# Differential attention one unit later, norms that share one root tile, and another order in the stage that rotates and norms the convolution

## The reference

```python
def diff_attention(q, k, v, lam):                       # layers 0 and 1 of the first block
    s = einsum('bqhpd,bkhpd->bhpqk', q, k) * 64 ** -0.5  # two score maps for each of 4 heads
    p = softmax(s, -1)
    a = p[:, :, 0] - lam * p[:, :, 1]
    return einsum('bhqk,bkhe->bqhe', a, v)
def rms_norm(x, w):
    return x * rsqrt(mean(square(x), -1) + eps) * w      # also with the mean taken off first (layer norm)

# first block, each layer
o = rms_norm(diff_attention(...), subln_w) * (1 - lam_init)      # per head of 128 features
# second block, layer 0 (even_mixer)
q = (rms_norm(cq, q_norm) @ w_uq).reshape(B, T, 8, 96)
kv = rms_norm(ckv, kv_norm) @ w_ukv
q, k = rms_norm(q, q_g), rms_norm(k, k_g)                        # per head of 96 features
q, k = rope on the last 32 features of each head
o_conv = silu(layer_norm(depthwise_conv(a * sigmoid(gate), dw_w) + dw_b, ln_g, ln_b))
# second block, layer 1 (odd_mixer)
q, k = rms_norm(q, q_g), rms_norm(k, k_g)                        # 8 heads of 64 features
y = head_group_norm(y0 + y1, gn_g, gn_b) * gate                  # with the mean taken off
```

## Time and profile before

| | |
|---|---|
| median of 3 runs | 3100.18 us (3095.39 to 3105.36) |
| profiled execution | 3105.21 us, span 3103.4 us |
| mean granted TensorE clock | 0.934 of full |
| busy | PE 2679.9 us (86%), DVE 1347.8 (43%), ACT 486.5 (16%) |
| DMA | 651.32 MB, mean 210 GB/s |

### The profile page before, as it was taken

How to read it: one execution, slowest core, us unless ns; L and a number is a source line. 1 busy time by engine, 2 the same in 40 slices (tenths; PEclk the granted TensorE clock), 3 DMA queues, 4 the chain that set the end, 5 groups by cost and what they waited for, 6 DMA issues and landing times. The chain is left out here.

```text
span 3103.4 us, 45313 instructions
## 1 busy us (share of the span) xinstructions
PE 2679.9 (86%) x19830; PEld 1647.8 (53%) x19830; DVE 1347.8 (43%) x2526; ACT 486.5 (16%) x1173; POOL 26.4 (1%) x48
## 2 busy tenths in 40 slices
PE   6988999999987999998969989879969787766665
PEld 3457844446766888735543334345449686423322
DVE  1774388543473876586321101121476763100001
ACT  1023200000222000235221001020051401100000
POOL 0000000000000000000000000000000000000000
PEclk8999999999998999998979999989989898878878
DMA  8530255332341666120239999981110026799998
GB/s 346 191 136 1 85 213 214 142 159 109 112 186 69 244 271 247 67 82 29 83 125 426 427 428 427 428 333 31 43 35 29 2 82 238 305 428 427 427 427 343
DMA packets 66357, 651.32 MB, mean 210 GB/s; under 512 B 14705, under 2 KB 25585, under 8 KB 26481
## 3 DMA queue, kind: packets, MB, share of 16 engines
q1 hardware_dynamic: 66160, 648.43, 51.9%
HBM read 644.08 MB, written 4.33 MB: 209 GB/s over the span
## 5 line engine op out<-in xcount | busy, mean ns | idle before, releaser
L369 PE MATMUL ps<-HT,ring 128*128 128x256 f32 (+1 forms) x3024 | 905.0, 460 | 27.2 <-DMA ring<-in_w_in 9.5
L369 PEld LDWEIGHTS ps<-HT,ring 128*128 128x128 f32 x3024 | 576.1, 192 | 330.9 <-issue 269.4
L2024 PE MATMUL ps<-ring,arena 128*32 128x256 f32 (+1 forms) x2976 | 371.9, 503 | 107.4 <-DMA ring<-in_moe_w 104.7
L442 DVE SCALAR_TENSOR_TENSOR acc<-ring,sil,acc 128x512 f32<-128x512 f32 x616 | 411.7, 744 | 0.0
L369 PE MATMUL ps<-arena,ring 128*128 128x256 f32 (+3 forms) x1232 | 372.3, 463 | 3.2 <-PEq L644 2.0
L2024 PEld LDWEIGHTS ps<-ring,arena 128*32 128x32 f32 (+1 forms) x2976 | 141.0, 130 | 315.8 <-issue 199.7
L369 PEld LDWEIGHTS ps<-arena,ring 128*128 128x128 f32 (+2 forms) x1232 | 230.2, 188 | 137.8 <-issue 118.0
L945 DVE SCALAR_TENSOR_TENSOR XT<-ps,modcols,XT 128x256 f32<-128x256 f32 x148 | 66.6, 481 | 358.3 <-PE ps L369 230.2
L2045 PE MATMUL ps<-ring,arena 128*32 128x256 f32 x960 | 89.9, 539 | 62.3 <-DMA ring<-in_moe_w 62.3
L2045 PE MATMUL ps<-ring,conv 128*64 128x512 f32 x512 | 116.1, 597 | 26.3 <-DMA ring<-in_moe_w 25.7
L369 PE MATMUL ps<-ring,HT 128*128 128x512 f32 (+1 forms) x288 | 105.1, 523 | 0.0
(11 more groups left out here) (379 smaller groups left out, 2618.6 us busy)
## 6 DMA issues: line engine op xcount, KB each, us to landing
ring<-in_moe_w SPq DMA_DIRECT2D x186, 2048.0 KB, 25.6
ring<-in_w_mod SPq DMA_DIRECT2D x24, 2048.0 KB, 8.2
ring<-in_ada_w SPq DMA_DIRECT2D x24, 2048.0 KB, 8.0
ring<-in_w_up SPq DMA_DIRECT2D x16, 2048.0 KB, 12.3
ring<-in_w_down SPq DMA_DIRECT2D x16, 2048.0 KB, 12.5
ring<-in_w_in SPq DMA_DIRECT2D x10, 2048.0 KB, 10.3
ring<-in_od_w_in SPq DMA_DIRECT2D x6, 2048.0 KB, 25.6
arena<-in_moe_w SPq DMA_DIRECT2D x10, 1024.0 KB, 8.0
```

The costliest lines, as they stand in the source:

```text
L369: last = nc.tensor.matmul(bank_of(job, j), lhsT, rhs, start=n == 0, stop=n == len(terms) - 1)
L442: ins = nc.vector.scalar_tensor_tensor(out=acc, in0=weights[:, k, :], scalar=s, in1=acc, op0=ALU.mult, op1=ALU.add)
L2024: last = nc.tensor.matmul(K.ps[M * j:M * j + M, 2 * (e % 2) + i, 0:FW], xs[:, e // 4 % 2, e % 4, 4 * h + k, :], weights((m, e, h), k, slic ...
```

## The change

1. Differential attention: the transposes, the copy out of PSUM, the values and the output copy of a unit each move one round later, and the order inside a round changes. PE: transposes of unit i-3, scores of unit i, values of unit i-4. ACT: copy of unit i-3, then exponentials of unit i. DVE: output of unit i-5. A wait of DVE on the exponentials of unit i-4 is dropped.
2. Norms: groups are gathered in batches (2, then up to 4 each; one each where the divisor differs). New constants `one_sums` and `pair_sums` (38 columns each, nonzero in columns 6 and 7) are cut at an offset, so that group j of a batch adds its sums into rows 2j and 2j+1 of each strip of one common tile. One square root and one reciprocal then serve the batch. A spread takes its row from 64 partitions instead of 128, and where the group has one sum per token it writes 128 output partitions at once instead of 64, so that 4 instructions spread 512 tokens where 8 did; the 512 columns lie in two half-used PSUM banks. On DVE the batch's last group is scaled after the next batch's reciprocal.
3. Rotation and convolution norm: PE packs the third pack before it adds the squares, and spreads the root before the last pack. ACT does its squares and the root before the first `keep`, and does two of the `keep`s after the SiLUs. DVE inverts before the third rotation and scales before the fourth.

The diff at its core:

```diff
-                half = grp["ones"][:, 48:80]
+                rows = grp["sums"][0:block.shape[0], 6 - row:38 - row]
...
-                for c in range(grp["src"][0].shape[1] // P):
-                    for h in range(2):
-                        pick = K.ident[:, 32 * c + 16 * h:32 * c + 16 * h + 1].broadcast_to([P, 64])
-                        last = nc.tensor.matmul(K.ps[64 * h:64 * h + 64, bank, c * P:(c + 1) * P], pick, rows, start=True, stop=True)
+                halves = 2 if grp["sums"] is K.pair_sums else 1
+                for c in (0, 2, 1, 3) if grp["src"][0].shape[1] == TT else (0, 1):
+                    tile = slice(c // 2 * 64, c // 2 * 64 + 64)
+                    for h in range(halves):
+                        at, m = 32 * c + row + h, P // halves
+                        last = nc.tensor.matmul(K.ps[m * h:m * h + m, 2 + 2 * (g % 3) + c // 2, c % 2 * P:(c % 2 + 1) * P],
+                                                K.ident[tile, at:at + 1].broadcast_to([64, m]),
+                                                rows[tile], start=True, stop=True)
...
+    if groups[0]["inv"] != groups[-1]["inv"]:
+        batches = [[g] for g in range(G)]
+    else:
+        batches = [list(range(min(2, G)))] + [list(range(g, min(g + 4, G))) for g in range(2, G, 4)]
...
+            for b in range(B + 1):
+                groups_before = batches[b - 1] if b else []
+                for g in groups_before[:-1]:
+                    scale(g)
+                if b < B:
+                    dve.wait_ge(*K.at("roots_done", b + 1))
+                    nc.vector.reciprocal(root[:, b % 4], root[:, b % 4]).then_inc(*K.inc("inverted"))
+                for g in groups_before[-1:]:
+                    scale(g)
...
-            for i in range(U + 3):
+            for i in range(U + 4):
+                if 3 <= i <= U + 2:
+                    j = i - 3
+                    pe.wait_ge(*K.at("probs_done", 2 * (j + 1)))
...
-                if i >= 3:
-                    j = i - 3
+                if i >= 4:
+                    j = i - 4
...
-                    if i >= 4:
-                        dve.wait_ge(*K.at("exps_done", 2 * (i - 3)))
...
             unpack(0)
+            pack(2)
             for b in range(4):
                 pe.wait_ge(*K.at("squares_act", b + 1))
                 add_up(b, sq[:, b, :]).then_inc(*K.inc("squares_summed"))
-            pack(2)
             unpack(1)
+            pe.wait_ge(*K.at("inverted", 1))
+            spread(root).then_inc(*K.inc("roots_spread"))
             pack(3)
             unpack(2)
-            pe.wait_ge(*K.at("inverted", 1))
-            spread(root).then_inc(*K.inc("roots_spread"))
             unpack(3)
```

More of the change, by code:

```diff
@@ new lines, in _ @@
+                    spread(g, 2 * g, means).then_inc(*K.inc("means_spread"))
+            for b, batch in enumerate(batches):
+                if b >= 2:
+                    pe.wait_ge(*K.at("roots_done", b - 1))
+                for j, g in enumerate(batch):
+                    if b and j == 2:
+                        spread_batch(b - 1)
+                    for i, s in enumerate(groups[g]["src"]):
+                        k = firsts[g] + i
+                        pe.wait_ge(*K.at("squares_" + sides[k], sides[:k + 1].count(sides[k])))
+                        add_up(g, row_of[g], sum_bank(b), sq[0:s.shape[0], k % 4, 0:s.shape[1]], k == firsts[batch[0]],
+                               k == firsts[batch[-1] + 1] - 1).then_inc(*K.inc("squares_summed"))
+                if b and len(batch) <= 2:
+                    spread_batch(b - 1)
@@ L691, in _, with take_roots @@
+            spread_batch(B - 1)
         @block.scalar
         def _(act):
+            def take_roots(b):
+                act.wait_ge(*K.at("squares_summed", firsts[batches[b][-1] + 1]))
+                if b >= 4:
+                    act.wait_ge(*K.at("roots_spread", batches[b - 4][-1] + 1))
+                grp = groups[batches[b][0]]
+                nc.scalar.activation(root[:, b % 4], K.ps[:, sum_bank(b), 0:P], ACT.Sqrt, bias=grp["eps"], scale=grp["inv"]).then_inc(*K.inc("roots_done"))
@@ L766, in _ @@
         def _(pe):
-            for i in range(U + 3):
+            for i in range(U + 4):
+                if 3 <= i <= U + 2:
+                    j = i - 3
+                    pe.wait_ge(*K.at("probs_done", 2 * (j + 1)))
+                    if j:
+                        pe.wait_ge(*K.at("probsT_done", j))
+                    for c in range(len(units[j]["v"])):
+                        last = nc.tensor.matmul(K.ps[:, 6, c * P:(c + 1) * P], E[:, j % nb, 0, c * P:(c + 1) * P], scaled_ident[:, j % 4],
+                                                start=True, stop=True)
+                    last.then_inc(*K.inc("transposed"))
                 if i < U:
@@ L1608, in scaled_norm_stage @@
     n = n_seg * T
-    norm_stage(K, [dict(src=[K.XT[:, k, 0:n] for k in range(KD)], ones=K.ones, inv=1.0 / D, eps=K.eps["rms"],
+    norm_stage(K, [dict(src=[K.XT[:, k, 0:n] for k in range(KD)], sums=K.one_sums, inv=1.0 / D, eps=K.eps["rms"],
                         out=[(K.HT[:, k, SEGS[s]], K.XT[:, k, SEGS[s]], SEGS[s], K.gain[:, s, k:k + 1], mod(K, which, s, k))
```

177 lines of the change are left out of this document (79 added, 98 removed).

## The result

The changed kernel takes 3092.5 us (median of 20 runs, 3087.6 to 3099.3), the kernel before 3100.2 us (20 runs beside them). The ratio is 0.9970, 95% interval 0.9962 to 0.9978: 9 us faster by the ratio (7.6 by the medians), where 26.8 were forecast. The direction was right; the time lies above the range. The profiled execution has a span of 3090.9 us, 12.5 less than before; that of before lay 5.0 us above its median, so part of the 12.5 is chance.

The account below looks back on a forecast made before the run. The last chain is DMA-led experts' work that starts earlier by whatever is saved before it. Terms sum to 26.8 us: 3105.2 becomes 3078.4, and 3073.4 us since that execution lay 5.0 above the median; range 3062 to 3087.

Parts of the forecast that it names:

- attention, layer 0: Differential attention, 16 units, 49.30 us: three steady heads at 0.8 and a shorter drain save 4.0 us (bounds 0, 5.5).
- attention, layer 1: Differential attention, 8 units, 33.48 us: later values shorten the drain and the third round, saving 3.2 us (bounds 1.5, 4.5).
- 16 groups: Norm of 16 groups, 29.04 us: shared reciprocals and shorter spreads, 3.8 us a batch, save 6.0 us (bounds 0, 8.5).
- four of 512: Norm of four groups of 512 tokens, 12.20 us: two of four reciprocals go, spreads halve; saves 2.2 us.
- four of 256: Norm of four groups of 256 tokens, 10.13 us: spreads no shorter; saves 1.2 us.
- low rank: Norm of low-rank inputs, 11.22 us, each group its own batch: earlier root, shorter first spread; saves 1.3 us.
- two with one group: Two norms with 512 tokens and one group: the one spread falls from 1.98 to about 1.0 us; saves 2.0 together.
- 8 groups: Norm of eight groups, 14.34 us: SP's wait for the move to DRAM limits the saving to 2.1 us at most.
- mean off: Norm with the mean off, 12.74 us: two reciprocals and a mean row four times narrower; saves 1.5 us.
- rotation: Rotation and convolution norm, 21.65 us: earlier root, SiLUs ahead of two `keep`s; ends 3.3 us earlier (bounds 1.5, 5).
- the fourth rival: Low clock outlives the norms into the attention behind the rotation stage, costing up to 50 us: 3123 us; chance 0.03.
- Rival 2: Norms leave PE less to do; 16 groups at 1.2 GHz lose 6, other norms 1 more: 3080 us; chance 0.12.

Follow-up runs that it names:

- before_warm: Kernel before plus the same unread products at the same places as in warm; 0.9967 of the kernel before, 3089.4 us.
- warm: Changed kernel plus unread 128x128 products: 5 at each norm's start, 2 ahead of and 2 behind its last spread, 10 in each differential attention; 0.9912, 3078.5 us.
- warm_again: warm run once more with no edit; 0.9942 of the kernel before, 3079.5 us.
- after_again: Changed kernel run once more with no edit; 0.9967 of the kernel before, 3088.2 us.
- warm_rotation: warm_output plus 5 unread products in the rotation and convolution norm, between the sums of squares and the unpack of group 1; 0.9907, 3072.9 us.
- warm_output: warm with VectorE's attention output copy right behind the same round's maxima, and no unread products in the two mean-off layer norms; 0.9924, 3076.1 us.
- unbatched: Changed kernel with each norm group in a batch of its own, spreads over 64 partitions kept; 1.0012 of the kernel before, 3104.5 us.
- unbatched_warm: unbatched plus the unread products of warm; 1.0018 of the kernel before, 3104.8 us.
- warm_ends: Changed kernel with only 2 unread products ahead of each norm's last spread and 2 behind it; 0.9963 of the kernel before, 3089.9 us.

## Why the prediction was wrong

The table has the terms of the sum; the change of each stage in the changed kernel's two traces; the same with filler in the changed kernel alone; and with filler in both kernels (`before_warm` against `warm`, or `warm_again` in two rows), with the clocks of the two. All in us.

| stage | forecast | after, after_again | filler in the changed one | filler in both (clocks) |
|---|---|---|---|---|
| attention, layer 0 | -4.0 | -0.7, -2.4 | -3.5 (`warm`) | -2.47 (1.00, 1.00) |
| attention, layer 1 | -3.2 | -1.9, -3.2 | -2.8 (`warm`) | -1.55 (0.95, 0.94) |
| 16 groups | -6.0 | -6.3, -6.4 | -7.6 (`warm`) | -9.20 (0.84, 1.00) |
| four of 512 | -2.2 | -1.3, -1.5 | -2.8 (`warm_again`) | -1.25 (1.00, 1.00) |
| four of 256 | -1.2 | -0.5, -0.2 | -1.9 (`warm`) | -0.39 (1.00, 1.00) |
| low rank | -1.3 | -1.1, -1.1 | -1.3 (`warm_again`) | -0.46 (1.00, 1.00) |
| two with one group | -2.0 | -0.8, -2.1 | -4.1 (`warm`) | -0.75 (0.83 and 0.86, 0.85 and 0.86) |
| 8 groups | -2.1 | -0.4, +0.5 | -2.1 (`warm`) | -2.02 (1.00, 1.00) |
| mean off | -1.5 | +0.9, +1.7 | -0.1 (`warm`) | -3.47 (0.72, 0.87) |
| rotation | -3.3 | -3.9, -2.9 | -4.3 (`warm_rotation`) | -3.94 (0.73, 0.86) |

Two steps failed. The first stands in the fourth rival and in the sum: "the dense stretches of before are back at full clock at once", and "no part is taken back later". The changed kernel spent 8.8 us at 1.2 GHz in the first norm (6.8 before) and 4.8 us more at the start of the out projection, 7.3 and 2.9 in the 8 groups and the start of the stage behind (3.4 and 0 before), 11.7 in the norm with the mean off (3.8 before). I worked out most stages at the clock of their old row. But the change takes work from TensorE in stages where it already waited, and there the clock went down with it; over all eleven stages the low-clock time stayed (89 and 91 us) while their length fell. The sentence on the dense stretches was wrong for the kernel before as well. I had read it from a mean; windows of before at the start of the out projection behind layer 1's norm, and of the attention behind the rotation stage, show 1.2 GHz:

```profile
954.14:959.14 5.00, 4.97 (x12) 4.02 (x13) 0.00 (x0) 2.56 (x8) 0.00 (x0) 0.50 0.02 5
1448.46:1454.46 6.00, 5.96 (x7) 2.52 (x8) 2.54 (x7) 2.84 (x5) 0.00 (x0) 0.50 0.00 0
```

Rival 2 named this mechanism, with 6 us in the 16 groups, which kept their clock (0.92), and 1 us for all other norms, in most of which it fell; even so it gave 3080, 12 us below the result.

The second step is the size of the terms. For the seven terms whose stages have a like clock in both kernels with filler (all rows but the 16 groups, the mean off and the rotation) the change is worth 8.9 us, where the sum had 16.0. The terms of both attentions and of all norms among them but the 8 groups came out at 0.3 to 0.6 of what I put. One reason shows: some savings were priced at 1.2 GHz, as the one spread of a one-group norm from 1.98 to 1.0 us; at a higher clock the old spread is shorter too, and less is left to save. For layer 1's attention and the norms of four groups no run says which part of my layout was too large. How the missing 18 us divide between the two steps stays open: the runs with filler in both kernels leave 8 to 17 us for the change, their stages 24.

The 16 groups came out at their 6.0 partly by luck: a batch cost 4.3 us and not 3.8, while their low-clock time halved (7.0 to 3.6 us), which the sum did not count on. In the same way the rotation stage was laid out at half clock and ran at 0.90 in the first trace (-3.9) and 0.70 in the second (-2.9).

Two terms were off for another reason as well. Layer 0's steady head came out at 10.40 us as laid out, but the drain saved nothing (9.55 us from a head's last long transposes to the end, 9.53 before): I let the values follow the transposes there, and they waited for VectorE's copy. With the copy moved, the stage reached 44.9. And the norm with the mean off stood still at -0.1 with filler in `warm`, since there the filler itself delays the means (4.07 us from the stage's start in `warm_output`, 3.62 in `warm`, 1.40 before); counted from the means to the end it takes 8.9 us in `warm_output`, 12.3 in the changed kernel and 11.3 before. Part of those 2.4 us is clock: the 32 records that spread the means took 3.61 us before and 1.96 in `warm_output`. That norm without filler at its start, and the clock held in another way, was not tried.

Right were: that savings reach the end, the pairing of 64-partition products, that two banks cost VectorE nothing, and, as lengths, the low-rank norm, the 16 groups and the rotation stage. One row was read wrong without harm: the four score records take 1.13 us, not 1.06.

The Trainium skill, "TensorE: Matmul & The Clock Gate", section "HAM oscillation — how this bites in real kernels", says that waits between groups of products make the clock fall again and again, and that the time at half clock costs half of itself. The traces agree in kind: in layer 0's attention and its norm `warm` had 12.2 us less of low clock than the changed kernel (3.5 instead of 6.9 + 8.8) and was 3.5 us shorter; half would be 6.1, but TensorE was not the bound all the time. The same page, "Part 1: The HAM clock gate (the "warmup" mystery)", says that the same kernel differs in this from run to run, as `after_again` did, and that for a forecast the ramp costs less than 1% of a typical span. Here the filler gave back 14 us of 3092 (the medians of the changed kernel and of `warm`), 0.5%, and yet more than the change gained.

## What to carry to other kernels

When TensorE waits in a stage, price the clock beside the work: look up the granted clock there and in the stage behind, and ask whether an edit that shortens TensorE's products lowers it. A few products that nobody reads, placed in waits that are there anyway, were worth more here (14 us) than the change itself (9 us). Give the same filler to the old kernel before its gain is put down to the change: there it was worth 10.7 us. Where a rule on the clock is needed, read it from windows at the start of each dense stage, not from the mean of the span. Two traces of one kernel differ by up to 2 us in a stage, so the sum of stages or the runs must decide.

## What the runs showed of the hardware

- TensorE with less to do was slower in doing it: with spreads cut from 1.09 to 0.57 us and VectorE unchanged, the 16 groups ran at 0.55 of the clock (`unbatched`, its slowest execution; 0.71 in `unbatched_warm`) instead of 0.88, and TensorE's busy time rose from 25.85 to 27.57 us.
- A dense stage behind a stage with waits began at 1.2 GHz: 4.8 us after the first norm of the changed kernel, none when four short products filled the norm's end (`warm_ends`).
- An unread product is no gift: at 1.2 GHz ten records of 128x128 took 2.39 us, at 2.4 GHz 1.35 us (`warm_output`), and where TensorE had work ready the stage paid for them.
